# Twelve conditioning vectors: products moved from GpSimd to TensorE column groups, all low parts to VectorE

## The reference, cut to what matters

```python
mod = jax.nn.silu(c) @ mod_w[l] + mod_b[l]      # (1024) @ (1024, 6 * 1024), for l = 0, 1
shift_m, scale_m, gate_m, shift_f, scale_f, gate_f = jnp.split(mod, 6, axis=-1)
# used in the last two blocks:
h = rms_norm(x, norm_mix_pre) * (1 + scale_m) + shift_m      # and likewise for the others
```

## Time and profile before

| | |
|---|---|
| median of 3 runs | 2698.08 us (2697.8 to 2703.37) |
| profiled execution, first to last instruction (span) | 2699.4 us |
| PE busy, DVE busy, ACT busy, POOL busy | 2440.6, 1856.6, 1194.6, 1029.9 us |
| mean granted clock of TensorE | 0.896 of full speed |
| read from memory over the span | 403 MB, 150 GB/s |

### The profile page before, as it was taken

One profiled execution on the slowest core, in us unless ns is written; L12 is line 12 of the kernel. 1 busy time (PEld: TensorE's weight loads), 2 busy tenths in 40 slices (PEclk: granted clock), 3 DMA queues, 4 the chain that ended last, 5 costly groups with the idle time before them and its releaser, 6 DMA issues.

```text
span 2699.4 us, 45800 instructions
## 1 busy us (share of the span) xinstructions
PE 2440.6 (90%) x17794; PEld 2347.4 (87%) x17794; DVE 1856.6 (69%) x2446; ACT 1194.6 (44%) x1720; POOL 1029.9 (38%) x501
## 2 busy tenths in 40 slices
PE   7998887998999999887898899898789799897998
PEld 7998777998998999877798899798677799897997
DVE  5667899766666666899975677573734488756555
ACT  5444342254444444443235444435323365543654
POOL 3655443054665566443125466221100122221222
PEclk9999898599999999999679999899655799998999
DMA  6665434045665565533214566343200155443552
GB/s 249 211 221 187 148 126 133 1 164 172 210 228 192 177 227 210 182 135 133 78 59 168 165 224 219 115 158 124 93 9 0 65 178 185 148 149 101 184 182 101
DMA packets 110412, 405.77 MB, mean 150 GB/s; under 512 B 12256, under 2 KB 12384, under 8 KB 109920
## 3 DMA queue, kind: packets, MB, share of 16 engines
q1 hardware_dynamic: 96192, 352.33, 38.5%
q0 software_dynamic: 13824, 50.34, 5.8%
q10 hardware_dynamic: 288, 1.57, 0.2%
HBM read 403.14 MB, written 1.05 MB: 150 GB/s over the span
## 4 chain that ended last, share of the span: by engine, by line
PE 66%; DVE 20%; issue 8%; POOL 3%; ACT 2%; DMA 0%; POOLq 0%; DVEq 0%; SPq 0%; ACTq 0%
PE bank L537 64%; DVE arena L1461 6%; DVE w_lo L1304 4%; PE bank L649 2%; POOL w_lo L467 1%; DVE arena L1506 1%; POOL mod_acc L502 1%; POOL mod_w_buf L494 1%; DVE arena L1511 1%; DVE rinv L1338 1%; DVE work L1342 1%; DVE work L1374 0%; DVE arena L1700 0%; DVE arena L1515 0%; DVE arena L1509 0%
## 5 line engine op out<-in xcount | busy, mean ns | idle before, releaser
L537 PE MATMUL bank<-h_hi,w_hi 128*128 128x256 f32 (+1 forms) x4016 | 1184.4, 295 | 124.2 <-DVE w_lo L1304 64.2
L537 PE MATMUL bank<-h_lo,w_hi 128*128 128x256 f32 (+1 forms) x4016 | 1160.8, 289 | 0.0
L537 PE MATMUL bank<-h_hi,w_lo 128*128 128x256 f32 (+1 forms) x4016 | 1159.4, 289 | 0.0
L467 POOL TENSOR_TENSOR w_lo<-w_raw,w_hi 128x1024 fp32r<-128x1024 f32 x221 | 551.7, 2496 | 1577.5 <-ACT w_hi L982 1576.9
L982 ACT ACTIVATE w_hi<-w_raw 128x1024 fp32r<-128x1024 f32 x663 | 700.1, 1058 | 784.7 <-PE bank L537 782.4
L537 PEld LDWEIGHTS bank<-h_hi,w_hi 128*128 128x128 f32 x4016 | 794.3, 198 | 144.2 <-DVE w_lo L1304 57.4
L1304 DVE TENSOR_TENSOR w_lo<-w_raw,w_hi 128x1024 fp32r<-128x1024 f32 x442 | 688.4, 1564 | 331.7 <-ACT w_hi L982 328.0
L537 PEld LDWEIGHTS bank<-h_lo,w_hi 128*128 128x128 f32 x4016 | 797.3, 199 | 5.7 <-issue 5.5
L537 PEld LDWEIGHTS bank<-h_hi,w_lo 128*128 128x128 f32 x4016 | 795.8, 198 | 0.0
L1461 DVE SCALAR_TENSOR_TENSOR arena<-arena,vecs 128x256 f32<-128x256 f32 x520 | 316.8, 672 | 0.0
L537 PE MATMUL bank<-hid_hi,w_hi 128*128 128x256 f32 x1056 | 297.9, 282 | 3.1 <-DVE hid_lo L1390 3.1
(11 more groups left out here) (205 smaller groups left out, 2093.2 us busy)
## 6 DMA issues: line engine op xcount, KB each, us to landing
w_raw<-weights SPq DMA_DIRECT2D x663, 512.0 KB, 3.4
mod_w_buf<-mod_w POOLq DMA_DIRECT2D x96, 512.0 KB, 4.0
tabs<-shape_tables SPq DMA_DIRECT2D x1, 1746.0 KB, 14.6
work<-v_bias ACTq DMA_DIRECT2D x2, 768.0 KB, 5.1
x<-x_fm SPq DMA_DIRECT2D x1, 1024.0 KB, 4.9
out_fm<-x SPq DMA_DIRECT2D x1, 1024.0 KB, 3.9
vecs<-vectors SPq DMA_DIRECT2D x1, 712.0 KB, 8.3
tabs<-shape_tables SPq DMA_DIRECT2D x1, 65.0 KB, 4.8
```

Source lines behind the costliest of these rows:

```text
L467: nc.gpsimd.tensor_tensor(w_lo[:, SPLIT - 1, :], w_raw[:, n % RAW, :], w_hi[:, SPLIT - 1, :].bitcast(F32), ALU.subtract).then_inc(lo_ready ...
L537: ins = pe.matmul(o, lhs, rhs, start=start, stop=stop, skip_group_check=share)
```

## The change

GpSimd computes nothing any more. It only issues the 96 loads of modulation weights, into three buffers, each when PE has used the one three places before. The low parts of all 663 weight tiles are made by DVE. PE computes the vectors itself: `silu(c)`, repeated 32 times, is the stationary operand (128 x 32), and the weights stream past as the moving one. A weight tile is cut into four blocks of 256 columns, and block j goes to the 32 columns of the array from 32j on, and so to the partitions from 32j on of one PSUM bank. So a tile is four float32 matmuls of 128 x 32 with 256 columns (`mod_tiles`), accumulated over the eight tiles of a vector. Then DVE copies the bank to `mod_rows` (`mod_copy`), and two matmuls with the table `pick` turn the rows into columns (`mod_cols`). The 96 tiles are given out by hand over PE's stream, in portions of 2, 3 and 6.

```diff
@@ GpSimd
-            def two_parts(part):
-                for k in range(2):
-                    acc = mod_acc[:, k, :]
-                    load(part + k, 0)
-                    load(part + k, 1)
-                    for kt in range(KT):
-                        low_part()
...
-                        nc.gpsimd.tensor_tensor(terms if kt else acc, terms,
-                                                c_act[:, kt:kt + 1].broadcast_to([P, TILE]), ALU.mult
-                                                ).then_inc(pool_link, 1)
-                        pool.wait_ge(pool_link, w.next(pool_link))
-                        if kt % 2 == 0:
-                            low_part()
-                        if kt:
-                            last = kt == KT - 1
-                            nc.gpsimd.tensor_tensor(acc, acc, terms, ALU.add
...
+            for n in range(DEPTH * MOD_PARTS * KT):
+                if n >= MOD_BUF:
+                    pool.wait_ge(mod_w_used, n - MOD_BUF + 1)
+                pool.dma_start(mod_w[:, n % MOD_BUF, :], mod_in[n]).then_inc(mod_w_full[n % MOD_BUF], 16)
@@ TensorE
-            def mod_part(b=3):
...
+            def mod_tiles(count, b=7):
+                for _ in range(count):
+                    n = state["mod"]
+                    part, kt = divmod(n, KT)
+                    state["mod"] += 1
+                    if n == 0:
+                        pe.wait_ge(c_ready, w.next(c_ready))
+                    if kt == 0 and part:
+                        pe.wait_ge(mod_ready, w.next(mod_ready))
+                    pe.wait_ge(mod_w_full[n % MOD_BUF], w.next(mod_w_full[n % MOD_BUF], 16))
+                    blocks = mod_w[:, n % MOD_BUF, :].rearrange("p (h j c) -> p j h c", h=2, j=4)
+                    for j in range(4):
+                        rows = slice(j * P // 4, (j + 1) * P // 4)
+                        mm(bank[b][rows, 0:2 * P].rearrange("p (h c) -> p h c", h=2), c_act[:, kt, :], blocks[:, j],
+                           kt == 0, kt == KT - 1, mod_w_used if j == 3 else None)
+                    if kt == KT - 1:
+                        pe.wait_ge(mod_w_used, n + 1)
+                        pe.sem_inc(mod_row_full, 1)
+            def mod_cols(b=7):
+                pe.wait_ge(mod_row_taken, w.next(mod_row_taken))
+                for h in range(2):
+                    mm(bank[b][:, 2 * P + 4 * h:2 * P + 4 * h + 4], mod_rows[:, h * P:(h + 1) * P], tab("pick"),
+                       sig=mod_col_full if h else None)
@@ TensorE, ffn(mod=False)
                 column_pair(h_ready, None)
+                if mod:
+                    mod_tiles(2)
                 column_pair(None, None)
+                if mod:
+                    mod_cols()
@@ TensorE, first_mixer
                     column_pair(h_ready if m == 0 else None)
+                    if m == 0:
+                        mod_tiles(2)
+                    if m == 1:
+                        mod_cols()
...
                     if i >= 1:
                         qk_stats(i - 1)
-                mod_part()
+                    if i in (QT // 2, QT - 3):
+                        mod_tiles(3, 3)
+                mod_tiles(2, 3)
...
-                mod_part(7)
+                    if i in (LN_VAR - 1, KT - 3):
+                        mod_tiles(3)
+                    if i == KT - 1:
+                        mod_tiles(2)
@@ TensorE, the order of the blocks
             for l in range(DEPTH):
                 mean_squares()
                 if l:
-                    mod_part()
-                ffn()
+                    mod_tiles(2)
+                    mod_cols()
+                    mod_tiles(6)
+                ffn(l > 0)
+                mod_tiles(3)
                 mean_squares()
-                mod_part()
+                mod_tiles(3)
                 first_mixer(l)
+                mod_tiles(3)
                 mean_squares()
-                mod_part()
-                ffn()
+                mod_tiles(3)
+                ffn(True)
+                mod_tiles(3)
                 mean_squares()
-                mod_part()
+                mod_tiles(3)
             for l in range(DEPTH):
                 mean_squares()
                 if l == 0:
-                    mod_part()
+                    mod_tiles(2)
+                    mod_cols()
+                    mod_tiles(6)
@@ VectorE, low_parts
-                    if n % SPLIT == SPLIT - 1:
-                        w.skip(hi_ready, 1)
-                    else:
-                        dve.wait_ge(hi_ready, w.next(hi_ready))
-                        v.tensor_tensor(w_lo[:, n % SPLIT, :], w_raw[:, n % RAW, :],
+                    dve.wait_ge(hi_ready, w.next(hi_ready))
+                    v.tensor_tensor(w_lo[:, n % SPLIT, :], w_raw[:, n % RAW, :],
@@ VectorE
+            def mod_copy(b=7):
+                dve.wait_ge(mod_row_full, w.next(mod_row_full))
+                v.tensor_copy(mod_rows[:, :], bank[b][:, 0:2 * P]).then_inc(mod_row_taken, 1)
@@ VectorE, the order of the blocks
             for l in range(DEPTH):
                 norm(vec("ffn1_norm", l, 0, KT))
                 if l:
+                    mod_copy()
                     mod_vector()
...
             for l in range(DEPTH):
+                if l == 0:
+                    mod_copy()
+                    mod_vector()
                 dve.wait_ge(mod_ready, w.next(mod_ready, MOD_PARTS))
                 norm(modv[:, l, 1, :], modv[:, l, 0, :])
```

More of the change, by code:

```diff
@@ L46 @@
 RAW = 6
+MOD_BUF = 3
 SPLIT = 3
@@ L392, in build @@
         c_ready = sem("c_activated")
[L393 to L394 removed]
+        mod_w_full = [sem(f"mod_weight_full{i}") for i in range(MOD_BUF)]
+        mod_w_used = sem("mod_weight_used")
+        mod_row_full = sem("mod_rows_in_psum")
+        mod_row_taken = sem("mod_rows_taken")
         mod_col_full = sem("mod_columns_in_psum")
@@ L531, in _ @@
             w = Count()
-            state = {"tile": 0, "pair": 0, "part": 0, "release": False}
+            state = {"tile": 0, "pair": 0, "mod": 0, "release": False}
             owed = [None, None]
@@ L756, in first_mixer @@
                     column_pair(gmix_ready if i == 0 else None, res_pair)
-            def mod_part(b=3):
-                p = state["part"]
-                state["part"] += 1
-                pe.wait_ge(mod_acc_ready, w.next(mod_acc_ready))
-                for c in range(KT):
-                    mm(bank[b][:, c:c + 1], mod_acc[:, p % 2, c * P:(c + 1) * P], tab("one"),
-                       sig=mod_col_full if c == KT - 1 else None)
+            def mod_tiles(count, b=7):
[21 more added lines that the diff above has]
+                       sig=mod_col_full if h else None)
             def recurrent_nsa_mixer():
                 column_pair(h_ready)
+                mod_tiles(2)
                 column_pair()
+                mod_cols()
                 column_pair()
@@ L1528, in first_mixer @@
                     some_taps(TAPS_Q if i < QT // 2 else TAPS_K)
-                    if i == QT - 2:
-                        mod_vector()
+                mod_copy(3)
                 v.reciprocal(q_root, q_root).then_inc(dve_link, 1)
@@ L1542, in first_mixer @@
                     some_taps(TAPS_V // 2)
+                    if i == 4:
+                        mod_vector(3)
                 for u in range(units):
@@ L1591, in first_mixer @@
                                 ).then_inc(csplit, 1)
-                mod_vector(7)
+                mod_copy()
                 for i in range(KT // 2):
```

88 lines of the change are left out of this document (26 added, 62 removed).

## The result

The changed kernel takes 2650.99 us (median of 4, 2650.19 to 2655.9), the kernel before beside it 2699.39 us (median of 4): a ratio of 0.9822, 95% interval 0.9808 to 0.9836. It is 48 us faster, where 22 were forecast: the direction and the range held, the size did not. The time is near that of the rival "all four groups at once", 2655 us, which had 0.17.

A forecast was written before the change was run, and what follows sets the result against it. PE was taken to bound the feed-forward loops, DVE the mixers' first stretch. 2699.4 plus 64 of costs less 86 of gains gave 2677 us for the span, 2676 us as the median; range 2645 to 2745.

The forecast's parts named there:

- all four groups at once: Rival: the four column groups run together, a modulation tile costs 0.43 us, the kernel takes 2655 us; chance 0.17.
- (d): Price of a modulation tile, four float32 matmuls of 256 columns on PE: 0.86 us, bounds 0.43 and 1.73 us.
- (a): Mixers' first stretches without GpSimd's share: 241 becomes about 205, 238 about 203 us; 71 us gained in all.
- (e): Tiles where PE is the bound: 28 x 0.86 = 24 us cost; those in q and k stages cost nothing.
- (b): Feed-forward loops: the lock costs little there; gain 5 us for the first loop, 3 for the others.
- (c): Output half of the mixers: gain 5 us for both, attention 2; bounds 0 and 15.
- (f): Starts and ends of modulation portions on PE: 9 us cost, bounds 0 and 20.
- (g): Four ordinary norms, three tiles ahead of the mean squares and three behind: 4 x 2.7 = 11 us cost.
- (h): Start of the second layer: `mod_cols` waits for `mod_copy` behind the norm, then six tiles before the loop; 15 us cost.
- (i): Start of the third block: norm 3 us late, six tiles end about 6 us after the first normed tile; 9 us cost.
- The groups don't overlap: Rival: column groups run one after the other, a modulation tile costs 1.73 us, the kernel takes 2742 us; chance 0.29.
- Low parts come late: Rival: PE waits for low parts in DVE's one queue, gain (a) is 35 instead of 71, 2715 us; chance 0.12.

The follow-up runs named there:

- more_same: The changed kernel with three more float32 matmuls of 248 columns per modulation tile, all in column group 0, results unread; 2722.85 us, 1.0077 of the kernel before.
- more_other: The changed kernel with three more float32 matmuls of 248 columns per modulation tile, one each in column groups 1, 2, 3; 2668.1 us, 0.9877 of the kernel before.
- moved: The changed kernel with the six modulation tiles of both long starts, and two tiles and the column behind them, moved to the q and k stages; 2636.08 us.
- low_paced: The kernel before with all low parts on VectorE, modulation on GpSimd, which keeps its 221 waits without the subtraction; 2680.39 us, 0.9931 of the kernel before.
- low_only: The kernel before with all low parts on VectorE and modulation left on GpSimd, without GpSimd's low-part waits; 2821.72 us, 1.0451 of the kernel before.

## Why the prediction was right or wrong

**The step that failed is (d), the price of a modulation tile**: "four steps of 0.216, **0.86 us** a tile". It measured 0.43 at full clock. The argument was that both records of one matmul need the same part of the array and that records start in the order of the program, so only the second record of one group could overlap the first of the next. The first half of that is so. What failed is the second: the order of the records is not group by group. The four first records start within 0.02 us and the four second ones 0.24 us later, so the groups are interleaved record by record, and no group waits for another; in more_same three groups even start ahead of records of group 0 that were issued before them. The earlier trace rows showed 11 records starting in half a microsecond where parts of the array change; the prediction took the weakest overlap that this allowed, and gave the right case 0.17.

**What hangs on it was also too large.** The forecast had 76 us for each us of price, more_other shows 41. Six tiles of a norm were charged at both sides of the mean squares; more_other's extra 0.42 us a tile lengthened three of the four ordinary norms by 1.26 us (9.45 became 10.71), which is 3 x 0.42, and the third, 10.69, not at all, since it had held a wait of 2.2 us for a load that is 0.2 in more_other: at most three of the six lie on the path. The eight tiles in each gate stage became 3.4 us dearer and the stage 1.1 us longer: the two portions of three took 1.26 us more each, the last two tiles none, and a wait of 1.4 us for a low part went.

**Step by step.**

- (a) Right: 71 us forecast for the mixers' first stretches, 35 and 34 measured in the windows (241 to 206, 238 to 204), 37.1 and 38.7 up to the end of their attention. Taps, low parts and rotations fell to the durations forecast. PE's waits for low parts, the doubt on which the lower bound and a rival stood, vanished. Its reasoning was partly wrong, and that the sum came out is in part luck: DVE at 190 is as forecast, but PE waits only 12 of the 206 us and so takes some 193 and not 176 + 7. With ten modulation tiles in it the 138 other matmuls must take nearer 40 than the 27 us put down for them, an estimate from these numbers. So PE is now the bound in the q and k stage, and the modulation tiles there are not covered, which (e) took for granted.
- (b) 5 us forecast for the first loop and 3 for the others. From first to last product the loops took 198.3, 191.9, 191.6 and 194.0 us and take 192.7, 194.6, 193.7 and 194.4: the first, the only one without modulation tiles in it, gives its 5; the others, with two tiles and the columns in each, lose 0.4 to 2.7 and show no gain of their own.
- (c) and (e). In each gate stage the two portions of three cost 1.5 us each (a weight tile of 4.40 us instead of 2.88), the last two tiles nothing (5.85 us with and without them). The stages are only 1.0 and 1.2 us longer, so about 2 us of gain lie under them, as (c) had it for the whole half: PE's waits for low parts there fell from 4.1 and 2.7 us to 1.4 and 1.4. Of (e)'s premise that eight tiles in the q and k stage cost nothing, see (a).
- (f) and (j). The 22 portions that end no vector cost 0.1 us each for the switch, the 12 that end one 0.35, if all are like those with products right behind them: 6 us for the 9 forecast. PE's waits for modulation loads are 22.3 us in 25 times, all but a few in the norms and long starts, where (g) to (i) had them. (j) can't be seen apart.
- (g) Forecast 11 us, or 5.8 at the measured price; measured 6.1.
- (h) Forecast 15, or 13 at that price; the gap grew by 14.2, with its six tiles at half clock and so at the forecast's 0.85. (i) Forecast 9, measured 8.4, with four tiles of six at half clock.

So the price carries 17 of the 25 us by the medians, perhaps a little more (more_other's profile has 3 us of the higher clock told of with moved). Where the rest lies, more_other's rows tell, since its tile has the forecast's price (the profiled run is 13 us below the forecast, the median 8). Against the table's last column they are 8 us lower in the two rows of the output half (+4.9 and +1.5 for 7.1 each), 2.6 in the first feed-forward loop, 2 in the third block, 1.5 in the mixers' first stretches (-36.1 and -35.3 for -35 each), and 5 are (f) and (j); the three rows of the second layer's start and the other feed-forward loops are together 5.4 higher. So (a) was right at that price too, and what was too high is above all the output half.

**Rivals.** "All four groups at once" came true, with its time. "The groups don't overlap" is refuted for this chip, but its sum was near: more_same, at 1.7 us a tile, takes 2723 us where it said 2742, and is slower than before. "Low parts come late" is refuted: PE's waits for DVE's low parts fell from 70.2 us to 18.4 over the span, and low_paced gains with the modulation still on GpSimd.

## What to carry to other kernels

When an engine's work is taken away, ask what its waits did for the others: GpSimd's low parts were slow, but they dealt out its other work over the weight tiles, and without their waits the same arithmetic cost 141 us. A small float32 product whose stationary side is 32 columns wide can be split over four column groups: here four such matmuls cost as much as one. And where modulation tiles must go on the engine that is the bound, they are worth putting in the middle of a stage with their loads long done, not at its start.

## What the runs showed of the hardware

Both records of four float32 matmuls in four column groups overlap, 0.43 us for 4 x 256 columns; three more in one group cost 1.26 us, in three groups 0.42. At a granted clock of 0.50, at the start of the second layer, the four took 0.85. The lock between VectorE and GpSimd was known to the prediction from the earlier trace rows; low_only shows how far it goes when GpSimd works without a pause: a pair of `h_lo` and `work` that needs 0.9 us takes 5.0. The Trainium skill says of the shared port pair (SBUF — State Buffer, SBUF: two separate sides) that it is an exclusive lock, held for a whole instruction; the trace of low_only agrees. A load of 512 KB on GpSimd's queue took 5.1 us to land in the changed kernel and 4.0 before, though GpSimd did nothing else; what makes it later was not tried.
